# Tables of the overflow blocks built in nine pieces instead of six, in a decoder block on one Trainium2 core

## The reference: what is computed

```python
logits = xn @ w_router + b_router
top_val, top_idx = lax.top_k(logits, 4); gates = softmax(top_val)
# per expert, on the tokens that chose it:
gate = minimum(h @ w_gate[e] + b_gate[e], 7.0)
up = clip(h @ w_up[e] + b_up[e], -7.0, 7.0)
y = ((up + 1.0) * gate * sigmoid(1.702 * gate)) @ w_down[e] + b_down[e]
# sum of y times its gate over a token's experts, residual, final norm
```

## Time and profile before

| | |
|---|---|
| median of 3 runs | 1583.55 us (1581.59 to 1583.69) |
| profiled execution, its own time | 1588.09 us |
| its span, and granted TensorE clock | 1586.4 us, 0.985 |
| PE busy | 1534.9 us, 97% |
| PEld busy | 1267.6 us, 80% |
| DVE busy | 1323.5 us, 83% |
| ACT busy | 1086.6 us, 68% |
| POOL busy | 598.5 us, 38% |
| DMA moved | 464.33 MB |
| chain of waits, by engine | PE 83%, DVE 11%, DMA 3%, issue 2%, ACT 1% |

### The profile page before, as it was taken

How to read it: one execution, slowest core, us unless ns; L and a number is a source line. 1 busy time by engine, 2 the same in 40 slices (tenths; PEclk the granted TensorE clock), 3 DMA queues, 4 the chain that set the end, 5 groups by cost and what they waited for, 6 DMA issues and landing times.

```text
span 1586.4 us, 29423 instructions
## 1 busy us (share of the span) xinstructions
PE 1534.9 (97%) x10453; PEld 1267.6 (80%) x10453; DVE 1323.5 (83%) x1458; ACT 1086.6 (68%) x1316; POOL 598.5 (38%) x371
## 2 busy tenths in 40 slices
PE   7999987889999999999999999999999999999997
PEld 6877767886888788878888888888888888888884
DVE  4256455554689999999999999999999999999996
ACT  4245431102477888877888888788888788888874
POOL 7000312101030224235555456545435555444553
PEclk9999998999999999999999999999999999999999
DMA  7321110001589999999999999999999999999994
GB/s 245 90 67 41 40 42 2 4 4 68 199 320 371 403 367 366 404 359 398 398 387 386 377 395 393 393 387 385 374 384 393 392 390 392 388 369 392 395 386 164
DMA packets 81275, 464.33 MB, mean 293 GB/s; under 512 B 11643, under 2 KB 12855, under 8 KB 33073
## 3 DMA queue, kind: packets, MB, share of 16 engines
q1 hardware_dynamic: 71424, 438.68, 70.2%
q0 software_dynamic: 9104, 24.52, 6.8%
q10 hardware_dynamic: 672, 0.07, 0.0%
HBM read 449.16 MB, written 23.13 MB: 298 GB/s over the span
## 4 chain that ended last, share of the span: by engine, by line
PE 83%; DVE 11%; DMA 3%; issue 2%; ACT 1%; POOL 0%; SPq 0%; POOLq 0%; ACTq 0%; DVEq 0%
PE banks L380 68%; DVE expert_w_lo L320 6%; PE banks L1839 5%; PE banks L2102 1%; PE banks L1932 1%; PE banks L2099 1%; DMA expert_w_raw<-in_moe_w_up_dram 1%; PE banks L1916 1%; PE banks L2037 1%; DMA gate_bias_rows<-in_moe_b_gate_dram 1%; PE banks L2084 1%; PE banks L2111 1%; ACT expert_w_hi L315 0%; DMA y_sums<-y_block,scatter_rows 0%; PE banks L2362 0%
## 5 line engine op out<-in xcount | busy, mean ns | idle before, releaser
L320 DVE TENSOR_TENSOR expert_w_lo<-expert_w_raw,expert_w_hi 128x1024 fp32r<-128x1024 f32 x764 | 908.2, 1252 | 31.1 <-ACT expert_w_hi L315 30.7
L315 ACT ACTIVATE expert_w_hi<-expert_w_raw 128x1024 fp32r<-128x1024 f32 x764 | 750.2, 1056 | 32.5 <-DMA expert_w_raw<-in_moe_w_down_dram 24.4
L380 PE MATMUL banks<-expert_w_hi,x_block_T_hi 128*128 128x512 f32 x1008 | 395.8, 393 | 2.1 <-DVE expert_w_lo L320 2.0
L380 PE MATMUL banks<-expert_w_lo,x_block_T_hi 128*128 128x512 f32 x1008 | 392.8, 390 | 0.0
L380 PE MATMUL banks<-expert_w_hi,x_block_T_lo 128*128 128x512 f32 x1008 | 392.5, 389 | 0.0
L742 POOL COPY scatter_gates<-slot_gate 128x1 f32 x26 | 225.5, 8674 | 249.3 <-DMA y_sums<-y_block,scatter_rows 249.3
L380 PEld LDWEIGHTS banks<-expert_w_hi,x_block_T_hi 128*128 128x128 f32 x1008 | 189.4, 188 | 43.1 <-DVE expert_w_lo L320 3.9
L380 PEld LDWEIGHTS banks<-expert_w_lo,x_block_T_hi 128*128 128x128 f32 x1008 | 189.2, 188 | 39.6
L380 PEld LDWEIGHTS banks<-expert_w_hi,x_block_T_lo 128*128 128x128 f32 x1008 | 189.3, 188 | 38.2
L380 PE MATMUL banks<-expert_w_hi,h_block_T_hi 128*128 128x512 f32 x528 | 209.4, 397 | 4.8 <-DVE expert_w_lo L320 4.2
L380 PE MATMUL banks<-expert_w_lo,h_block_T_hi 128*128 128x512 f32 x528 | 206.1, 390 | 0.0
(11 more groups left out here) (397 smaller groups left out, 1975.8 us busy)
## 6 DMA issues: line engine op xcount, KB each, us to landing
expert_w_raw<-in_moe_w_up_dram SPq DMA_DIRECT2D x128, 1024.0 KB, 7.9
expert_w_raw<-in_moe_w_down_dram SPq DMA_DIRECT2D x128, 1024.0 KB, 9.7
expert_w_raw<-in_moe_w_gate_dram SPq DMA_DIRECT2D x126, 1024.0 KB, 10.1
w_raw<-in_w_in_dram SPq DMA_DIRECT2D x24, 512.0 KB, 3.7
residual<-in_x_dram SPq DMA_DIRECT2D x8, 512.0 KB, 5.1
w_raw<-in_w_out_dram SPq DMA_DIRECT2D x8, 512.0 KB, 3.3
staged_raw<-in_moe_w_gate_dram SPq DMA_DIRECT2D x2, 1024.0 KB, 6.0
y_sums<-residual SPq DMA_DIRECT2D x4, 512.0 KB, 7.4
```

Source lines behind the costliest of these rows:

```text
L315: act.activation(self.hi[:, k % self.nhl, 0:width], self.raw[:, slot, 0:width], ACT.Copy)\
L320: dve.tensor_tensor(self.lo[:, k % self.nhl, 0:width], self.raw[:, (k - self.staged) % self.nraw, 0:width], self.hi[:, k % self.nhl, 0:wid ...
L380: last = pe.matmul(o, lhs, rhs, start=start and t == 0, stop=stop and t == 2, skip_group_check=preset)
```

## The change

`LOOP0` becomes 10, so blocks 1 to 9 are written out on VectorE, TensorE and GpSimd, and the work of the six pieces is spread over nine. Old piece 1 is cut in two, old piece 2 in two (with one operation of the old piece 3 moved behind its sum), the one-hot of old piece 4 in two halves of 128 x 1024 that each give a `pairs_ok`. The last piece, which reads the slot sums, goes to block 9 and behind split k17 instead of k13. TensorE's slot sums go to block 9 with it, still in front of k12.

```diff
-    LOOP0 = 7
+    LOOP0 = 10
             lo(8, 14)
-            if isinstance(i, int):
+            if isinstance(i, int) and i < LOOP0 - 1:
                 over_part(i)
-            lo(14, 21)
+            lo(14, 18)
+            if isinstance(i, int) and i == LOOP0 - 1:
+                over_part(i)
+            lo(18, 21)
...
                     ch.link(dve.reduce_sum(nbl[:, :], nbv[:, :, :].rearrange("p b e -> p e b"), AXX))
+                elif i == 2:
                     ch.link(dve.tensor_tensor_scan(bend[:, :], onesf[:, :], nbl[:, :], 0.0, ALU.mult, ALU.add))
...
-                elif i == 2:
+                elif i == 3:
                     ch.link(dve.tensor_tensor(dovr[:, :, :], OH[:, :, :, :].rearrange("p t k e -> p (t k) e"),
                                               bc(over[:, :], [P, NP, NE], 1), ALU.mult))
+                elif i == 4:
                     ch.link(dve.reduce_sum(dover[:, :], dovr[:, :, :], AXX))
-                elif i == 3:
+                    ch.link(dve.tensor_scalar(dfull[:, :], dest[:, :], 1.0 / P, (-ROW0 - (P - 1) / 2) / P, ALU.mult, ALU.add))
+                elif i == 5:
                     MAGIC = 1.5 * 2.0 ** 23
-                    ch.link(dve.tensor_scalar(dfull[:, :], dest[:, :], 1.0 / P, (-ROW0 - (P - 1) / 2) / P, ALU.mult, ALU.add))
...
-                elif i == 4:
-                    dve.tensor_tensor(ohR[:, :, :], bc(destr[:, :], [P, NP, P], 2), bc(iotaR[:, :], [P, NP, P], 1),
+                elif i in (6, 7):
+                    ms = slice((i - 6) * (NP // 2), (i - 5) * (NP // 2))
+                    dve.tensor_tensor(ohR[:, ms, :], bc(destr[:, ms], [P, NP // 2, P], 2), bc(iotaR[:, :], [P, NP // 2, P], 1),
                                       ALU.is_equal).then_inc(S("pairs_ok"), 1)
-                elif i == 5:
+                elif i == 8:
...
-                        pe.wait_ge(S("pairs_ok"), TT + 2)
+                        pe.wait_ge(S("pairs_ok"), TT + 3)
```

## The result

| | before | after | ratio |
|---|---|---|---|
| median of 20 runs each | 1581.83 us | 1585.99 us | 1.0029 (1.0016 to 1.0043) |
| profiled execution, its own time | 1588.09 us | 1591.65 us | |
| its span | 1586.4 us | 1589.9 us | |

The change makes the kernel 0.29% slower, 4.6 us; I had forecast 3.05 us less. The time lies outside my range.

What follows compares the result with a forecast made beforehand. PE was taken as the bound, 34.51 us per undisturbed block. Savings 0.75 + 0.67 + 2.73 less losses 0.1 and 1.0 gave 3.05 us off the median: 1580.6 us, range 1578.4 to 1583.6.

Steps and rivals of the forecast that it cites:

- Block 5: Its 34.51 us interval was taken as undisturbed; its piece shrinks from 1.42 to 1.04 us, saving 0.
- block 9: Slot sums return on PE there, with flip and refilling: 1.0 us lost; VectorE doesn't wait for them.
- block 6: VectorE's wait for the slot sums goes, its piece becomes 1.13 us: 2.73 us saved, bounds 2.3 and 2.73.
- block 4: Its piece shrinks from 2.20 to 0.9 us, within the 0.91 limit: 0.67 us saved, bounds 0.3 and 0.67.
- Block 3: Smaller piece shortens PE's wait at split k23: 0.75 of 1.45 us saved, bounds 0.5 and 1.45.
- Block 8: Its 1.42 us piece is 0.05 over the first limit: 0.1 us lost, bounds 0 and 0.6.
- rival A: Stretch stays on split k23, pieces over 0.91 us show in blocks 5 to 8: gain only 1.6 us, 1581.9; chance 0.17.
- Block 2: VectorE's gain is waited away for block 3's gate bias, behind a DMA backlog: 0, bounds 0 and 0.3.
- the three written-out blocks: Three more blocks written out, three fewer looped: jumps cost PE at most 0.1 us, so the term is 0.
- Rival D: Code of blocks 7 to 9 fetched afresh through weight-filled queues, PE between 695 and 800 us: slower, 1591.3 us; chance 0.06.
- B: Transfers set the pace and hand waits back, ScalarE waiting over 1 us behind block 3: gain 0.6, 1583.0; chance 0.10.
- C: Cutting piece 1 loads block 2's weights 1.1 us earlier: 1579.4 us; sign, block 2's interval under 38; chance 0.17.

Runs made afterwards that it cites:

- experiment 5: Changed kernel, TensorE's code shifted by 57 instructions, a pair of no-effect waits in each of 57 chunks from block 1 on; 1578.06 us, ratio 0.9982 to the kernel before.
- experiment 1: Changed kernel with 114 no-effect waits at the start of TensorE's program, shifting its code by 57 instructions; 1582.91 us, ratio 1.0021 to the kernel before.
- experiment 4: Changed kernel with its last piece back behind split k13 in block 9; ratio 1.0043 to the kernel before.
- experiment 7: Changed kernel without TensorE's If and the loop over overflow blocks in it; 1579.54 us, ratio 0.9989 to the kernel before.
- experiment 11: experiment 5 with the loads of the final gain and down biases moved behind SP's loop; 1576.94 us, ratio 0.9972 to the kernel before.
- experiment 8: Blocks 1 to 9 written out but the old six pieces kept, with the same 57-instruction shift as experiment 5; 1581.58 us, ratio 1.0004 to the kernel before.
- experiment 6: Kernel before, shifted by 199 instructions in the chunks so TensorE's loop lies in its packets as in the changed kernel; 1589.87 us, ratio 1.0055.
- experiment 9: Kernel before, shifted by 115 instructions in the chunks of the written-out blocks; profiled only, no timed comparison, blocks 30 to 31 took 37.43 us.
- experiment 10: Kernel before, shifted by 150 instructions in the chunks of the written-out blocks; profiled only, no timed comparison, blocks 30 to 31 took 40.52 us.

## Why the prediction was wrong

**Right, by its steps.** Block 5's undisturbed 34.51 us was the measure, and block 7's 0 and block 9's loss of 1.0 (measured 1.06) came as written; block 6 lost its 2.73 and block 4 its 0.67 to within 0.01. Block 3 gave back all of its 1.45 where I took 0.75; in the profile of experiment 5 it gave 0.8. Block 8 lost nothing (0.1 forecast). Block 5 lost 0.2 where I had 0. The siblings with the same pieces (experiments 1, 4, 5, 7 and 11) show that blocks 4 and 5 were near the edge: block 4 kept 0 to 0.67 there and block 5 lost 0 to 0.8, so the step for block 4 was some 0.3 too hopeful on the whole. Block 5's loss is of rival A's kind: in experiments 1, 5, 7 and 11 PE stands 0.18 to 0.25 us in it, just behind a split that was stretched to 2.18 us while GpSimd spread the up bias. VectorE didn't wait for the slot sums, and experiment 4 measures what that wait cost. The half of the one-hot took what the row of a split had promised, 1.21 us:

```profile
701.66 1.21 DVE L1782 TENSOR_TENSOR onehot_row<-dest_row,iota_rows 128x1024 bf16<-128x1024 f32 x1
```

Experiments 5 and 8 put these pieces at 3.5 us in timed runs, against the 3.05 of the sum; in their profiles the blocks 3 to 10 differ by 1.8 us (244.2 against 246.0), between the changed kernel and the one before by 3.6.

**Block 2.** I set it to 0, because what VectorE wins there it waits for the bias row of block 3. In the changed kernel's profile that wait was 5.3 us against the 2.96 of the earlier trace rows, and the interval grew by 3.11. That this is the change isn't shown: with the old pieces the interval is 35.5 to 38.3 in seven profiles, with the new ones and the loads in their old place 35.4 to 41.4 in five, one execution of each. Nor does coming early to block 1 explain it (4.46 us here): experiments 5 and 6 came still earlier and took 37.1 and 37.5. It stays open.

**The step that failed** is the one on the three written-out blocks: "the loop's jumps cost PE at most 0.1 us and leave nothing to win". The row was read rightly (but for its 1008 matmuls being two per chunk, not one), and asked the wrong question. It shows that the jumps of this layout leave PE next to no idle time. I took from it that jumps cost nothing, while the change moves TensorE's code by 969 instructions and so redraws which jump finds its target at hand. In place of 0 this term measured 4.6 to 6.9 us for the branch, and with the slow restart 5.7 to 8.7 us in the interval, in all five profiles with this layout or one like it.

Rival D had the right kind, code that is fetched through queues full of weights, and the right sign, but the wrong place: I looked for it in the new blocks between 695 and 800 us, where every interval was 34.51 but the one with the slot sums, and gave it 0.06. Its own argument against it, that blocks 2 to 6 are written out and lose nothing, holds for code that runs in order. It says nothing of the one place where the engine leaps over 350 instructions.

The Trainium skill's rule (Runtime: NRT & Kernel Launch, "Instruction fetch mechanics"), that a taken branch to code outside the window waits for a fetch, was the one that I set aside for the row. The trace agrees with it at the `If`, 6.86 us against 0.36, and experiment 7 shows it by taking the branch away. With packets that begin 0.43 in by my count, the rule's window, the packet in hand and the next, also fits all twelve forward jumps; the loop's own jump, 351 instructions back, never waited (0.22 to 0.25 us in every looped block of the thirteen profiles). I had read it only as a reason to gain by unrolling; it speaks against any edit that moves code in front of a jump.

**Other rivals.** A is out for blocks 6 to 8, none of which is longer than 34.62 us in any profile with the new pieces; what block 5 lost, 0 to 0.8 where A gave 0.13, is of its kind. B is out: the longest wait of ScalarE for weights between blocks 3 and 9 is 0.5 us in both profiles. C didn't come: cutting piece 1 in two didn't shorten block 2, and its sign, an interval under 38, shows in five of the seven profiles with the old pieces too, so it could decide nothing. Fewer transfers in block 2's way may help, as the one profile of experiment 11 has it; its time can't be told apart from that of experiment 5.

## What to carry to other kernels

An edit that changes how much code stands in front of a loop changes, besides its own work, where each jump lands; if the time moves and the blocks concerned don't, look at the duration of the branches behind the loops in the sequencer's rows before anything else. A wait that the profile puts down to an instruction long done is the sign. Test it by shifting the code alone, with no-effect instructions where the sequencer has time, in the new kernel and in the old: a layout that costs 8.7 us, as in experiment 6, can hide or fake any gain of 3.

## What the hardware showed unexpectedly

- A branch over 350 instructions took 0.36 us or 4.6 to 6.9 us on TensorE, by the place of the code alone. The five that waited had the target two 16 KB packets on from the branch, the seven others in the next packet, if packets begin where the stop of experiment 9 puts them; between experiments 9 and 10, with 35 instructions more, the wait is there in full.
- The packet came on the instruction queue 2.2 to 4.5 us behind the start of the branch in all twelve profiles, waited for or not, and took 0.9 to 1.0 us. A branch that waited ended 1.4 to 1.5 us behind the packet's end. The changed kernel's branch was the longest because its packet came last, 4.5 us on; in the four others that waited it was 2.2 to 2.5.
- The 57 instructions with waits on a reached constant at the start of TensorE's program took 0.11 us each, from 3.0 to 9.2 us. The first matmul came only 1.55 us later, because PE had waited for its input up to 7.66 us in any case; with 64 it was 2.3 us. One per chunk in the expert stage cost nothing: those intervals stayed at 34.51 where the pieces allow it.
- The profiled executions of the thirteen kernels reach block 1 between 471.3 and 482.0 us, with little edited in front of it but those waits. What sets that isn't settled; it is larger than the effect of the change, which is why it took the marks to see it.
